# Sixteen shift/scale weight units with places of their own, half of them unsplit, and two query tiles interleaved

## What is computed

```python
mod = (jax.nn.silu(cond) @ ada_w + ada_b).reshape(cond.shape[0], N_MOD, 1, D_MODEL)
sh1, sc1, gt1, sh2, sc2, gt2 = [mod[:, i] for i in range(N_MOD)]
h = rms_norm(x, norm_g[0]) * (1 + sc1) + sh1
z = h @ w_in            # queries, keys, values, gates and the other mixers
```

## Time and profile before

| | us |
|---|---|
| median of 3 runs (886.43 to 888.51) | 886.71 |
| the profiled execution | 886.34 |
| its span, first to last instruction | 884.6 |

### The profile page before, as it was taken

One profiled execution on the slowest core, in us unless ns is written; L12 is line 12 of the kernel. 1 busy time (PEld: TensorE's weight loads), 2 busy tenths in 40 slices (PEclk: granted clock), 3 DMA queues, 4 the chain that ended last, 5 costly groups with the idle time before them and its releaser, 6 DMA issues.

```text
span 884.6 us, 13033 instructions
## 1 busy us (share of the span) xinstructions
PE 827.9 (94%) x4891; PEld 730.3 (83%) x4891; DVE 526.2 (59%) x763; ACT 350.6 (40%) x555; POOL 86.4 (10%) x118
## 2 busy tenths in 40 slices
PE   3769998899999999899999999999999999999996
PEld 1569998788886488758999999999999967888785
DVE  2872285667766574877655555555545565444854
ACT  3772342113110143856434434244343433334542
POOL 2630012111120022430000000000000000000000
PEclk8879998899999999999999999999999999999998
DMA  9863127356450658435322231322223054332652
GB/s 298 281 182 84 47 62 194 107 80 165 120 152 7 206 195 250 143 104 159 90 77 71 71 90 53 95 71 71 71 71 90 29 171 138 130 131 96 207 203 90
DMA packets 99950, 109.54 MB, mean 124 GB/s; under 512 B 6999, under 2 KB 79863, under 8 KB 99655
## 3 DMA queue, kind: packets, MB, share of 16 engines
q1 hardware_dynamic: 94103, 95.77, 35.3%
q0 software_dynamic: 3952, 11.53, 5.2%
q10 hardware_dynamic: 1856, 1.71, 0.7%
HBM read 106.19 MB, written 2.82 MB: 123 GB/s over the span
## 4 chain that ended last, share of the span: by engine, by line
PE 71%; DVE 6%; DMA 2%; issue 2%; ACT 2%; ACTq 0%; DVEq 0%; SPq 0%
PE PAIR L1529 43%; PE PAIR L1706 21%; PE PAIR L1485 3%; DMA RAW<-in_ada_w_dram 2%; DVE WLO L1029 1%; ACT WHI L790 1%; PE PAIR L1666 1%; DVE T L1386 1%; PE PAIR L1661 1%; PE PAIR L1518 1%; PE PAIR L1510 1%; DVE ASLO L1354 0%; PE PAIR L1500 0%; PE PAIR L1642 0%; DVE X L1394 0%
## 5 line engine op out<-in xcount | busy, mean ns | idle before, releaser
L1529 PE MATMUL PAIR<-Hhi,WHI 128*128 128x320 f32 x960 | 227.3, 316 | 4.5 <-DVE Hlo L1369 3.5
L1529 PE MATMUL PAIR<-Hhi,WLO 128*128 128x320 f32 x960 | 225.1, 313 | 0.0
L1529 PE MATMUL PAIR<-Hlo,WHI 128*128 128x320 f32 x960 | 225.0, 313 | 0.0
L1029 DVE TENSOR_TENSOR WLO<-RAW,WHI 128x1024 fp32r<-128x1024 f32 (+1 forms) x115 | 141.6, 1241 | 66.4 <-ACT WHI L790 62.3
L1529 PEld LDWEIGHTS PAIR<-Hhi,WHI 128*128 128x128 f32 x960 | 164.6, 192 | 6.9 <-issue 6.4
L1529 PEld LDWEIGHTS PAIR<-Hlo,WHI 128*128 128x128 f32 x960 | 164.9, 192 | 0.0
L1529 PEld LDWEIGHTS PAIR<-Hhi,WLO 128*128 128x128 f32 x960 | 164.5, 192 | 0.0
L790 ACT ACTIVATE WHI<-RAW 128x1024 fp32r<-128x1024 f32 (+1 forms) x115 | 118.8, 1048 | 37.6 <-DMA RAW<-in_ada_w_dram 16.2
L1706 PE MATMUL PAIR<-WHI,ASHI 128*128 128x512 f32 x300 | 95.3, 399 | 5.7 <-DVE ASLO L1354 3.9
L1706 PE MATMUL PAIR<-WHI,ASLO 128*128 128x512 f32 x300 | 94.6, 397 | 0.0
L1706 PE MATMUL PAIR<-WLO,ASHI 128*128 128x512 f32 x300 | 94.5, 396 | 0.0
(11 more groups left out here) (218 smaller groups left out, 835.8 us busy)
## 6 DMA issues: line engine op xcount, KB each, us to landing
RAW<-in_ada_w_dram SPq DMA_DIRECT2D x48, 512.0 KB, 4.4
RAW<-in_ffn_up_dram SPq DMA_DIRECT2D x44, 512.0 KB, 3.8
RAW<-in_ffn_down_dram SPq DMA_DIRECT2D x44, 512.0 KB, 3.3
RAW<-in_w_in_dram SPq DMA_DIRECT2D x20, 512.0 KB, 5.0
RAW<-in_w_out_dram SPq DMA_DIRECT2D x16, 512.0 KB, 5.5
WE<-weight_rows POOLq DMA_DIRECT2D x20, 128.0 KB, 3.9
out_dram<-X SPq DMA_DIRECT2D x5, 512.0 KB, 5.0
X<-in_x_sample_dram POOLq DMA_DIRECT2D x4, 512.0 KB, 7.6
```

The lines of the kernel that those rows point to most:

```text
L1029: dve.tensor_tensor(WLO[:, u % RING, 0:w], RAW[:, u % RING, 0:w], WHI[:, u % RING, 0:w].bitcast(F32), ALU.subtract).then_inc(lo_split, 1)
L1529: last = pe.matmul(t[:, 512 * half:512 * half + HALF], w[:, n_or_slot, cols(k)], h[:, k, HALF * half:HALF * half + HALF], start=(k == 0 an ...
```

## The change

The twelve units u4 to u15 get places of their own: ten in the memory of `Hhi` and `Hlo` (40 KB per partition, empty until the operand is made), two in `GATE`, each with a semaphore of its own; u0 to u3 and everything from u16 on use the ring. Of the 16 units those with n % 4 in (1, 2) are no longer split; PE multiplies them from where they land in plain fp32, as it does the gate rows. `HEAD_STEPS` is reordered, the goals of the opening are written out, u16 and u17 are split after the last "rows" step, and x tiles 2 and 3 are issued ahead of the position tables, the constants together after u7. The two query tiles are made together, chunk by chunk. In the diff, the first change after `if at_ == len(HEAD_STEPS)` is ScalarE's, the next VectorE's; the change in the loop with `UPTO[s] - n + q` is in PE's `split_rows`.

```diff
-HEAD_STEPS = [("xs", 0), ("ad", 0), ("xs", 1), ("consts", 0), ("ad", 1), ("xt", 0), ("rows", 0), ("xs", 2), ("xt", 1),
-              ("ad", 2), ("xs", 3), ("xt", 2), ("rows", 1), ("xs", 4), ("ad", 3), ("xt", 3), ("rows", 2), ("xt", 4),
+HEAD_STEPS = [("xs", 0), ("ad", 0), ("xs", 1), ("ad", 1), ("consts", 0), ("rows", 0), ("xt", 0), ("xs", 2), ("xt", 1),
+              ("ad", 2), ("rows", 1), ("xs", 3), ("xt", 2), ("xs", 4), ("ad", 3), ("rows", 2), ("xt", 3), ("xt", 4),
               ("rows", 3)]
+HEAD_UNITS, HEAD_GOALS = 16, [4, 4, 8, 8, 8, 8, 8, 12, 12, 12, 12, 16, 16, 16, 16, 16, 16, 16, 16]
...
+        HALL, _ = at("HALL", [P, 10, D], F32, h_at)
...
+        def in_area(n):
+            return RING <= n < HEAD_UNITS
+        def raw_at(n, w=D):
+            if in_area(n):
+                a = n - RING
+                return HALL[:, a, 0:w] if a < 10 else GATE[:, a - 10, 0:w]
+            return RAW[:, n % RING, 0:w]
+        def ring_before(n):
+            m = n - RING
+            while in_area(m):
+                m -= RING
+            return m
...
         def raw_unit(n):
-            return UNITS[n][0] == "ada"
+            return UNITS[n][0] == "ada" or n < HEAD_UNITS and n % 4 in (1, 2)
...
+        for at_, n in enumerate(HEAD_GOALS):
+            goal[at_] = n
...
             def load(n):
+                if in_area(n):
+                    (o, a, b, src), = source(UNITS[n])
+                    sp.dma_start(raw_at(n).rearrange("p (a b) -> p a b", a=a), src).then_inc(area_in[n - RING], 16)
+                    return
                 wait_raw(n)
...
                 if n == 3:
+                    for g in (2, 3):
+                        sp.dma_start(XS[g], x_tile[g]).then_inc(x_in[g], 16)
                     for h in range(2):
                         sp.dma_start(POSC[64 * h:64 * h + 64, :], pos_col).then_inc(pos_in, 16)
                         sp.dma_start(POSR[64 * h:64 * h + 64, :, :], pos_row[h].partition_broadcast(64)).then_inc(pos_in, 16)
-                    for g in (2, 3):
-                        sp.dma_start(XS[g], x_tile[g]).then_inc(x_in[g], 16)
-                elif RING <= n < RING + 2:
-                    for dst, src in consts[4 * (n - RING):4 * (n - RING) + 4]:
+                elif n == 2 * RING - 1:
+                    for dst, src in consts:
                         sp.dma_start(dst, src).then_inc(consts_in, 16)
...
                 if at_ == len(HEAD_STEPS):
+                    split_to(HEAD_UNITS + 2)
                     act.wait_ge(mod1, 1)
...
                         wait_copied(dve, ("xt", g))
+                    split_to(HEAD_UNITS + 1)
                     modulate(1)
                     for k in range(KC):
...
                             .then_inc(h_lo, 1)
+                        split_to(HEAD_UNITS + 2)
...
                     u = UPTO[s] - n + q
+                    first, end = q == 0, q == n - 1
+                    if raw_unit(u):
+                        wait_raw_in(pe, u)
+                        for k in range(per):
+                            last = pe.matmul(t[0:4, 0:w], COND[:, per * q + k, :], raw_at(u)[:, w * k:w * k + w],
+                                             start=first and k == 0, stop=end and k == per - 1)
+                        last.then_inc(filled[USE[s][0]] if end else ada_used, 1)
+                        continue
                     wait_split(pe, u)
...
+            def first_tiles():
+                steps = [("q", i) for i in range(2)]
+                tiles = [wait_free(pe, s) for s in steps]
                 for k in range(KC):
-                    if wait_h:
-                        pe.wait_ge(h_lo, k + 1)
+                    pe.wait_ge(h_lo, k + 1)
+                    for s, t in zip(steps, tiles):
+                        if k == 0:
+                            wait_split(pe, UPTO[s] - 1)
+                        slot = (UPTO[s] - 1) % RING
+                        for n, (w, h) in enumerate(((WHI, Hhi), (WHI, Hlo), (WLO, Hhi))):
+                            for half in range(2):
+                                last = pe.matmul(t[:, 512 * half:512 * half + HALF], w[:, slot, cols(k)],
+                                                 h[:, k, HALF * half:HALF * half + HALF],
+                                                 start=(k == 0 and n == 0), stop=(k == KC - 1 and n == 2))
+                        if k == KC - 1:
+                            last.then_inc(filled[USE[s][0]], 1)
```

More of the change, by code:

```diff
@@ L223, in sem @@
             return ctx.enter_context(nc.semaphore(name))
+        h_at = place["at"]
         Hhi = sb("Hhi", [P, KC, TOK], F32R)
@@ L338, in hybrid_trunk_layer @@
         raw_in = [sem(f"raw_in{i}") for i in range(RING)]
+        area_in = [sem(f"area_in{i}") for i in range(HEAD_UNITS - RING)]
         hi_split, lo_split = sem("hi_split"), sem("lo_split")
@@ L413, in wait_copied, with wait_raw_in @@
             eng.wait_ge(drained[USE[key][0]], USE[key][3])
-        def raw_count(n):
-            return 16 * sum(2 if UNITS[m][0] == "vg" else 1 for m in range(n % RING, n + 1, RING))
+        def in_area(n):
[10 more added lines that the diff above has]
+            return m
+        def raw_count(n):
+            return 16 * sum(2 if UNITS[m][0] == "vg" else 1 for m in range(n % RING, n + 1, RING) if not in_area(m))
+        def wait_raw_in(eng, n):
+            if in_area(n):
+                eng.wait_ge(area_in[n - RING], 16)
+            else:
+                eng.wait_ge(raw_in[n % RING], raw_count(n))
         def width(n):
@@ L553, in wait_raw @@
             def wait_raw(n):
-                m = n - RING
+                m = ring_before(n)
                 if m >= 0 and is_split(m):
@@ L787, in split_to @@
                         continue
-                    act.wait_ge(raw_in[u % RING], raw_count(u))
+                    wait_raw_in(act, u)
                     wait_slot(act, u)
-                    act.activation(WHI[:, u % RING, 0:width(u)], RAW[:, u % RING, 0:width(u)], ACT.Copy)\
+                    act.activation(WHI[:, u % RING, 0:width(u)], raw_at(u, width(u)), ACT.Copy)\
                         .then_inc(hi_split, 1)
@@ L1028, in split_to @@
                     w = width(u)
-                    dve.tensor_tensor(WLO[:, u % RING, 0:w], RAW[:, u % RING, 0:w], WHI[:, u % RING, 0:w].bitcast(F32),
+                    dve.tensor_tensor(WLO[:, u % RING, 0:w], raw_at(u, w), WHI[:, u % RING, 0:w].bitcast(F32),
                                       ALU.subtract).then_inc(lo_split, 1)
@@ L1520, in piece2, with channel_tile @@
                 last.then_inc(filled[USE[key][0]], 1)
-            def channel_tile(t, n_or_slot, wait_h=False, part=(0, 1)):
+            def first_tiles():
+                steps = [("q", i) for i in range(2)]
+                tiles = [wait_free(pe, s) for s in steps]
                 for k in range(KC):
-                    if wait_h:
-                        pe.wait_ge(h_lo, k + 1)
+                    pe.wait_ge(h_lo, k + 1)
[10 more added lines that the diff above has]
+                            last.then_inc(filled[USE[s][0]], 1)
+            def channel_tile(t, n_or_slot, part=(0, 1)):
+                for k in range(KC):
                     for n, (w, h) in enumerate(((WHI, Hhi), (WHI, Hlo), (WLO, Hhi))):
@@ L1569, in mix @@
                     last.then_inc(filled[USE[s][0]], 1)
-                elif kind in FEATURE:
+                elif s == ("q", 0):
+                    first_tiles()
+                elif kind in FEATURE and s != ("q", 1):
                     u = UPTO[s] - 1
@@ L1573, in mix @@
                     wait_split(pe, u)
-                    channel_tile(t, u % RING, s == ("q", 0)).then_inc(filled[USE[s][0]], 1)
+                    channel_tile(t, u % RING).then_inc(filled[USE[s][0]], 1)
                 elif kind == "v":
```

## The result

The changed kernel takes 892.43 us (median of 8 runs, 888.33 to 896.05) where the kernel before takes 887.38 beside it (8 runs, 886.43 to 888.51): ratio 1.0051, interval 1.0028 to 1.0073. It is slower by 0.5%, outside the range of the forecast (887.2, up to 891.2). The profiled execution is the shortest of the 8: 888.33 us, span 886.6. That matters for the reading: its trace shows the new opening at its best.

What follows compares the result with a forecast made beforehand. The prediction took TensorE (71% of the chain) as the bound, the change touching only the opening: query tiles start 0.7 us later, the key tile 0.5 later, so 886.71 becomes 887.2 us; range 882.5 to 891.2.

Steps and rivals of the forecast that it cites:

- The step that failed: Opening, second and third groups of four shift/scale units on PE: 37.6 to 43.0 and 46.2 to 51.6 us, full clock.
- rival 1: PE's clock falls ahead of the second "ad" group, costing 1.95 us: 889.2, or 891.1 if the third too; chance 0.30.
- The rule of the Trainium skill that was weighed: Transposes don't count as PE activity like matmuls, so the clock would fall before the second "ad" group: about 2 us more.
- u4, the start of ad1: Fifth shift/scale unit lands at about 21.4 us, is split, and PE starts the first "ad" group at 23.8 us.
- ad1's half clock: After idling, PE runs the first "ad" group at the low clock for about 3.9 us, until 27.7 us.
- An "ad" group at full clock: Two split and two unsplit shift/scale units on PE go from 3.7 to 5.4 us.
- The tail: From the end of the third "ad" group to the first query tile: shrinks from 10.7 to 9.1 us.
- A change of that moment is a change of the whole time: When PE finishes the two query tiles, about 76.3 us before, any shift carries fully into the kernel's time.
- the 74.8 us of SP's waits: SP's queue waited 74.8 us, 20 times, for VectorE's low parts; given as the reason DMA was half empty at 40-44 us.
- The interleaving: Two query tiles made together fill only waits for Hlo, about 0.2 us; the pair takes 16.0 us, 60.7 to 76.7.
- Rival 2: The opening follows its weights' landings, not the lists; third "ad" group ends at 44.8, 6.8 us sooner: 880.4 us; chance 0.22.
- rival 3: Only the interleaving acts on the path; PE keeps the old schedule and saves 0.2 us: 886.5 us; chance 0.08.

Runs made afterwards that it cites:

- again: The changed kernel, unedited, run and profiled a second time: 895.3 us, ratio to the kernel before 1.0040.
- pair_only: The kernel before with the two query tiles made together and nothing else of the change: 889.67 us, ratio 0.9983.
- the single fills: Three edits of the changed kernel, filler matmuls in the gaps, ahead of the first "ad" group, or ahead of the query tiles: 890.59, 890.37, 888.07 us.
- goals_fill: The changed kernel with splits moved ahead of copies in the lists, plus filler matmuls at three places: 881.05 us, ratio to the kernel before 0.9914.
- fill_all: The changed kernel with the fillers of all three single fills together: 887.53 us, ratio to the kernel before 0.9962.
- before_fill: The kernel before with fillers ahead of the constants' transposes, the last column products and the first query tile: 888.07 us, ratio 0.9990.
- fill_front: The changed kernel with 30 filler matmuls ahead of the first "ad" group only: 890.37 us, ratio to the kernel before 0.9990.
- split_goals_fill: As goals_fill, but with all 16 units split: 885.21 us, ratio to the kernel before 0.9959.
- before_again: The kernel before, unedited, profiled a second time: one run of 884.37 us.
- before: The kernel before, unedited, in its first trace; 887.38 us beside the changed kernel's first runs.

## Why the prediction was wrong

**The step that failed** is the one that lets both groups run at full clock: "PE begins ad2 at 37.6 us and ends it, 5.4 us on, at 43.0", "ad3 begins at 46.2 and ends at 51.6". The fall there was left to rival 1. It stands in one of two traces, in both groups, at 1.6 us each where the rival had 1.95 (3.0 us up to k0's copy), and with fillers in the gaps it is gone and 3.8 us with it (known to 2.7). The rule of the Trainium skill that was weighed ("TensorE: Matmul & The Clock Gate", Part 4, PE-mode transpose) agrees with the second trace and not with the first: same instructions, same idle pieces ahead of ad2 (0.93 and 1.4 us) and ad3 (1.1), another outcome. In ad2 the clock fell 0.6 us after the group had begun at full pace. The forecast treated as a property of the schedule what is a property of an execution; that the trace of before had kept the clock over one such stretch and lost it over another was the hint.

**The sizes of the other terms** are read from the first trace of the change. First query matmul: forecast 60.7, measured 62.76.
- u4, the start of ad1: 23.8 forecast, 24.41 measured (+0.6). Its high part began at 21.76 instead of 21.4, and its low part took 1.51 us (22.85 to 24.36), not 1.23.
- ad1's half clock: 3.9 us forecast, from q0. The two unsplit units took 5.21 us, 3.60 at full clock; at half clock half of the time is lost, so 1.61 lost are 3.2 us, and the clock rose at 29.6, 5.2 us after the start (+0.7).
- An "ad" group at full clock: 5.4 forecast, 5.75 measured (39.19 to 44.94, 48.12 to 53.87); each change between split and unsplit form takes some 0.1 us more than the pace. Three groups: +1.0.
- The tail: 9.1 forecast, 8.9 measured (53.87 to 62.76): -0.2.

The low part of u4 ran beside GpSimd's sums of positions (last section). Together +2.1. The pair then takes 16.3 us (62.76 to k0's first matmul at 79.02), 16.0 forecast. So without a fall k0's copy is 3.0 us later than in the trace of before, with both falls 6.0 (89.39 in the trace of `again`); the ratio of 1.0051 makes 4.5 us of 887.38, between the two. The forecast had 0.5 us at this point, so the mis-sized terms make 2.5 us of the miss, without any fall, and two falls 3.0 more. By the sizes alone the time would be near 889.7 us (an estimate, 887.2 and 2.5), inside the range; it takes the falls to leave it. That a fall is the usual case is inferred from this, and from the granted clocks of the runs.

**A reading that was too strong.** "A change of that moment is a change of the whole time": behind k0's copy the traces differ by up to 9.4 us (798.1 to 807.5), so one trace's milestone is not one execution's time. And the 74.8 us of SP's waits were read as the opening's; 21.7 of them are.

**What was right.** Transfers: u15 by 41.0 (41.6 forecast), SP's waits gone from the head. The path goes by the lists and not by the landings: both groups wait for VectorE's low part, at 1.4 us and 1.1 us of idle, as worked out, each later than forecast by what was lost before it. u16 and u17 stand in front of the modulation (57.80 to 59.70). An unsplit unit takes what the earlier trace rows gave, 1.76 us at full clock (two in 3.60 us, with the last one's end). The interleaving is worth nothing measurable (`pair_only`). Rival 2 is refuted by the starts of ad2 and ad3, rival 3 by the result.

**What stays open.** Why the clock falls in one execution and not in the next under the same instructions. (The Trainium skill, "TensorE: Matmul & The Clock Gate", Part 1, "What's actually happening", tells of the same from run to run at a kernel's start, and puts it to the phase of a free-running monitor. The two traces agree that it differs from run to run; no run here shows the phase.) Why the single fills and `goals_fill` measure more than their traces show. Whether the changed opening beats the old one when both have their clock: `fill_all` (0.9962) and `before_fill` (0.9990) overlap, and the latter lost its clock elsewhere. Only with the goals moved too is the changed opening clearly ahead (`goals_fill`, 0.9914). Whether the places of their own are needed for that: no run moves the splits in the kernel before.

## What to carry to other kernels

Earlier transfers are worth nothing where an engine's list, not the landing, sets the start: move the split ahead of the copy in the list first, and look for the idle piece that goes. Where PE has nothing but transposes, two-column products and short idle pieces for some microseconds (6.5 ahead of ad2 here), its clock is part of the cost of a schedule, so profile more than one execution before calling such a stretch harmless. Cheap matmuls of ones in the gaps are a test of that in one edit, and here a remedy.

## What the runs showed of the hardware

- The clock is not fixed by the instruction order: the same kernel has 1.00 and 0.63 in the same window of two executions. The length of one idle piece doesn't fix it either. A piece of 1.65 us behind 6.86 us of fillers left it up (`fill_front`, ad1 whole at full clock). Behind pieces of 1.77 us (`goals_fill`) and 2.17 us (`split_goals_fill`) in the same place it fell, 1.1 and 0.6 us into ad1. One of 2.35 us, ahead of 32.73, left it up in `before_again` (1.00 from 32 to 44 us).
- Fillers in one place don't hold the clock in the next: in `fill_front` it fell in ad2 and ad3, in `before_fill` from 33.4 us. That they move a fall is not shown, since it fell in these stretches without fillers too: `again` in ad2 and ad3, `pair_only` at 38 us (0.75 from 36 to 40), `before_again` at 45.8 (0.72 from 44 to 48), where `before` had 1.00 in both windows.
- Some operations of VectorE and GpSimd hold each other up. In `split_goals_fill` four low parts took 8.13 us (2.03 each, 1.23 in the earlier trace rows), and GpSimd's sum of positions beside them 2.28 where the one before took 1.27. In the changed kernel two low parts from 37.81 took 2.45 us together, so nothing extra; there it was GpSimd's select beside them that took 1.26 us (37.94), where one of the same size just ahead of them took 0.29 (37.50). The Trainium skill, "SBUF — State Buffer", "SBUF: two separate sides", states such a lock for VectorE operations with two SBUF inputs against GpSimd operations that read SBUF; the rows agree, and no run here took GpSimd's sums away to prove it.

```profile
21.73 1.27 POOL L679 TENSOR_TENSOR XSA<-XSA,POSC 128x512 f32<-128x512 f32 x1
22.62 8.13 DVE L1062 TENSOR_TENSOR WLO<-HALL,WHI 128x1024 fp32r<-128x1024 f32 x4 [5.89 <-ACT WHI L822]
22.96 2.28 POOL L678 TENSOR_TENSOR XSB<-XSB,POSR 128x512 f32<-128x512 f32 x1
```
